# A hybrid attention layer on one core: gate rows by sums on VectorE, and another order of the first loads

## The reference, cut to what matters

```
shift, scale, gate = split(silu(cond) @ w_ada + b_ada, 3)     # cond: c_ctx for context, c for latents
h = rms_norm(x, g_norm) * (1 + scale) + shift
z = h @ w_in                                                  # q, k, v, g of both mixers
oa = differential attention, 8 heads: (softmax1 - lam * softmax2) @ v
ob = grouped-query attention, 8 heads, q and k RMS-normalised
o  = concat(rms_norm(oa) * silu(ga), ob * silu(gb))
y  = rms_norm(x + gate * (o @ w_out), g_final)
```

## Time and profile before

| | us |
|---|---|
| median of 3 runs | 1323.68 (1323.24 to 1323.74) |
| the profiled execution | 1324.19, span 1322.3 |
| TensorE matmul busy in the span | 1267.9 |
| VectorE busy | 717.7 |
| ScalarE busy | 601.9 |
| GpSimd busy | 217.0 |

### The profile page before, as it was taken

How to read it: one execution, slowest core, us unless ns; L and a number is a source line. 1 busy time by engine, 2 the same in 40 slices (tenths; PEclk the granted TensorE clock), 3 DMA queues, 4 the chain that set the end, 5 groups by cost and what they waited for, 6 DMA issues and landing times.

```text
span 1322.3 us, 19007 instructions
## 1 busy us (share of the span) xinstructions
PE 1267.9 (96%) x7399; PEld 1017.3 (77%) x7399; DVE 717.7 (54%) x1155; ACT 601.9 (46%) x1265; POOL 217.0 (16%) x374
## 2 busy tenths in 40 slices
PE   2699999999999999999999999999999999999996
PEld 1466666788888888888888787878788787888885
DVE  1444441855647657456565656565666766523343
ACT  1322312454555545555555545555555656322123
POOL 2000110301202003022122222121213322200001
PEclk9999999999999999999999999999999999999998
DMA  9999784211212112131212222221213431433234
GB/s 300 359 354 350 272 270 161 65 47 50 68 49 84 33 53 88 49 91 53 78 57 78 73 63 71 60 81 57 86 49 108 126 108 64 150 121 135 80 135 159
DMA packets 144216, 156.57 MB, mean 118 GB/s; under 512 B 8008, under 2 KB 122792, under 8 KB 143360
## 3 DMA queue, kind: packets, MB, share of 16 engines
q1 hardware_dynamic: 137232, 132.19, 31.1%
q0 software_dynamic: 6896, 23.17, 5.5%
HBM read 144.18 MB, written 11.16 MB: 117 GB/s over the span
## 4 chain that ended last, share of the span: by engine, by line
PE 88%; DVE 5%; DMA 3%; SPq 2%; ACT 1%; issue 1%; POOL 0%; ACTq 0%; DVEq 0%
PE z_ps L542 23%; PE z_ps L544 22%; PE z_ps L543 22%; PE ring L637 5%; PE ring L738 5%; PE ring L672 3%; PE ring L740 2%; PE ring L562 2%; SPq L455 1%; DMA x_sb<-in_x_sample_dram 1%; PE ring L764 1%; PE ring L544 1%; PE ring L543 1%; PE ring L542 1%; DMA ada_raw<-in_w_ada_dram 1%; DMA w_raw<-in_w_in_dram 1%
## 5 line engine op out<-in xcount | busy, mean ns | idle before, releaser
L542 PE MATMUL z_ps<-w_hi,xt_hi 128*128 128x512 f32 x1360 | 567.5, 417 | 2.4 <-DVE xt_lo L1270 1.0
L544 PE MATMUL z_ps<-w_hi,xt_lo 128*128 128x512 f32 x1360 | 533.2, 392 | 0.0
L543 PE MATMUL z_ps<-w_lo,xt_hi 128*128 128x512 f32 x1360 | 531.5, 391 | 0.0
L1126 DVE TENSOR_TENSOR w_lo<-w_raw,w_hi 128x512 fp32r<-128x512 f32 x272 | 191.6, 707 | 249.0 <-ACT w_hi L814 247.0
L814 ACT ACTIVATE w_hi<-w_raw 128x512 fp32r<-128x512 f32 x272 | 170.4, 627 | 335.0 <-PE z_ps L544 322.2
L542 PEld LDWEIGHTS z_ps<-w_hi,xt_hi 128*128 128x128 f32 x1360 | 256.1, 188 | 69.9 <-issue 23.7
L544 PEld LDWEIGHTS z_ps<-w_hi,xt_lo 128*128 128x128 f32 x1360 | 255.5, 188 | 56.9
L543 PEld LDWEIGHTS z_ps<-w_lo,xt_hi 128*128 128x128 f32 x1360 | 257.4, 189 | 37.8
L922 ACT ACTIVATE s_sb<-s_sb,small 128x768 f32<-128x768 f32 (+1 forms) x120 | 97.9, 820 | 2.8 <-DVE small L1206 2.8
L1206 DVE TENSOR_REDUCE small<-s_sb 128x2 f32<-128x1536 f32 (+1 forms) x60 | 88.3, 1471 | 18.7 <-ACT s_sb L814 17.5
L738 PE MATMUL ring<-v_hl,pt_hi 128*128 128x256 f32 x400 | 96.2, 324 | 0.0
(11 more groups left out here) (147 smaller groups left out, 1257.4 us busy)
## 6 DMA issues: line engine op xcount, KB each, us to landing
w_raw<-in_w_in_dram SPq DMA_DIRECT2D x208, 256.0 KB, 3.1
ada_raw<-in_w_ada_dram SPq DMA_DIRECT2D x64, 512.0 KB, 8.8
w_raw<-in_w_out_dram SPq DMA_DIRECT2D x64, 256.0 KB, 3.5
gate_pt<-in_w_ada_dram SPq DMA_DIRECT2D x12, 512.0 KB, 6.6
gate_sg<-in_w_ada_dram SPq DMA_DIRECT2D x12, 512.0 KB, 5.4
o_spill<-row_st POOLq DMA_DIRECT2D x14, 320.0 KB, 3.1
row_st<-o_spill POOLq DMA_DIRECT2D x14, 320.0 KB, 3.4
x_sb<-in_x_sample_dram SPq DMA_DIRECT2D x4, 1024.0 KB, 13.6
```

The costliest lines, as they stand in the source:

```text
L542: pe.matmul(out, hi_l, hi_r, start=start, stop=False)
L543: pe.matmul(out, hi_l, lo_r, start=False, stop=False)
L544: return pe.matmul(out, lo_l, hi_r, start=False, stop=stop)
L1126: dve.tensor_tensor(w_lo[:, b, :], w_raw[:, kg // 2 % RAW_RING, kg % 2, :], w_hi[:, b, :].bitcast(F32), ALU.subtract).then_inc(w_lo_done, 1)
```

## The change

It does two things.

1. *Order of the first loads.* SP issues the five token tiles first, then modulation weights 0 to 3. TensorE transposes the tokens of step 0 before its first modulation products, and VectorE normalises the tokens before it handles the first modulation rows. GpSimd issues the `lam` tables only when six slices of `xt_lo` are done and the norm and rotation tables when twelve are; the work on them on ScalarE and VectorE moves from step 3 to step 8 and, for the norm weight, step 15.

2. *The gate.* The 64 products of passes 0 and 1 go. The gate columns are loaded in passes 6 to 12 by GpSimd, two buffers of 512 KB, into the half of the work area that mixer A leaves unused (the tiles q, k, v, pt are laid out by halves for that). In steps 4, 9, 11 and 13 VectorE multiplies 512 columns by a column of silu(cond) and adds them to `gate_acc`, once for each of the two rows: `gate_sums`, 64 parts of two instructions, ten parts in a pass (`GATE_STEPS`). What then lies over 128 partitions is summed by eight products at the end of step 0 of pass 13 (`step_gate`); the bias is added in step 1 of that pass, where before it was pass 2. The bias is loaded in pass 5 instead of pass 1. Two waits of ScalarE and VectorE on the gate's bank in pass 2 go.

```diff
-GATE_SLOT = KT - 3
-GATE_END = 2 * KT - 1
-GATE_RING = 8
+GATE_COLS = D_MODEL // 2
+GATE_LOADS = 2 * KT
+GATE_STEPS = [4, 4, 9, 9, 11, 11, 13, 13, 13, 13]
+GATE_FROM = 4
+GATE_SUM_IT = OUT_IT
...
+def gate_parts():
+
+    out, i = {}, 0
+    for it in range(D_IT + 1, GATE_SUM_IT):
+        for s in GATE_STEPS:
+            if i < 2 * GATE_LOADS and (it, s) >= (D_IT + 1, GATE_FROM):
+                out.setdefault((it, s), []).append(i)
+                i += 1
+    return out
...
-            for n in range(4):
-                load_ada(n)
             for t in range(TILES):
                 src = x_prompt[0] if t == 0 else xs_v[:, t - 1, :]
                 sp.dma_start(x_sb[:, t, :], src).then_inc(x_in[t], 16)
+            for n in range(4):
+                load_ada(n)
+            load_w(0)
             load_ada(4)
-            load_w(0)
             load_w(1)
...
-            def step_gate(s):
+            def step_gate():
+
                 n = TURN["GATE"]
-                bank = claim(n) if s == GATE_SLOT else RB(n)
-                for m in gate_pieces(s):
-                    k, u = divmod(m, 2)
-                    pe.wait_ge(gate_in[m % GATE_RING], 16 * (m // GATE_RING + 1))
-                    for jj in range(2):
...
+                bank = claim(n)
+                pe.wait_ge(sel_set, 4)
+                pe.wait_ge(gate_summed, 2 * GATE_LOADS)
+                for r in range(2):
+                    for j in range(4):
+                        ins = pe.matmul(bank[32 * j:32 * j + 2, :], gate_sel[:, r, :],
+                                        gate_acc[:, r, NCOL * j:NCOL * (j + 1)], start=(r == 0), stop=(r == 1))
+                filled(ins, n)
+
+            h_transpose(0, 0)
             for quarter in range(4):
                 modulation(0, quarter)
             columns(0)
-            h_transpose(0, 0)
             h_transpose(0, 1)
...
+            def gate_sums(i):
+
+                m, piece = divmod(i, 2)
+                k, u = divmod(m, 2)
+                dve.wait_ge(gate_in[u], 16 * (k + 1))
+                if k:
+                    dve.wait_ge(gate_summed, i - 3)
+                raw = gate_raw[:, u, NCOL * piece:NCOL * (piece + 1)]
+                c0 = GATE_COLS * u + NCOL * piece
+                for r in range(2):
+                    acc, weight = gate_acc[:, r, c0:c0 + NCOL], cs[:, KT * r + k:KT * r + k + 1]
+                    if k == 0:
+                        ins = dve.tensor_scalar(acc, raw, weight, None, ALU.mult)
+                    else:
+                        ins = dve.scalar_tensor_tensor(acc, raw, weight, acc, ALU.mult, ALU.add)
+                ins.then_inc(gate_summed, 1)
...
-                    if it == G_IT + 1 and s == 0:
+                    if (it, s) == (GATE_SUM_IT, 1):
                         gate_rows_out()
+                    for i in GATE_PARTS.get((it, s), []):
+                        gate_sums(i)
...
+            pool.wait_ge(h_lo, KT // 2 - 2)
             for i, v_ in enumerate((lam_q1, lam_q2, lam_k1, lam_k2)):
                 pool.dma_start(lam_raw[:, i, :], v_.rearrange("a h d -> a (h d)").broadcast_to([P, H_A * DK_A])
                                ).then_inc(lam_in, 16)
+            pool.wait_ge(h_lo, KT - 4)
...
+                    for i in past:
+                        if i % 2 and i // 2 + 2 < GATE_LOADS:
+                            pool.wait_ge(gate_summed, i + 1)
+                            load_gate(i // 2 + 2)
+                    past = GATE_PARTS.get((it, s), [])
```

## The result

The changed kernel takes 1335.0 us (median of 4 runs, 1334.6 to 1335.7) against 1323.7 (4 runs, 1323.2 to 1324.1) of the kernel before on the same chip: ratio 1.0085, interval 1.0072 to 1.0098. It is 11.3 us slower; 6.1 were forecast. The profiled execution took 1335.7 us with a span of 1333.8. Further down, one of four executions of `e3_even` had a granted clock of 0.56 throughout and took 2080 us, and the times given for that run are those of the other three.

What follows compares the result with a forecast made beforehand. A start set by loads, then TensorE's own queue, was taken to bound the kernel. The terms -21.2 + 1.6 + 3.7 - 1.2 + 2.0 - 5.0 + 25.2 + 1.0 gave +6.1 us: 1329.8 on the median, range 1323 to 1337.

Steps and rivals of the forecast that it cites:

- passes 6 to 12: VectorE's gate sums delay pt_lo and TensorE waits: 2.8 us in pass 6, 3.8 each in 7 to 11, together +25.2.
- pass 13: Eight last gate products cost +2.0 us; four additions ahead of v_lo and q_lo on VectorE cost +1.0.
- The gate groups: Passes 0 and 1: dropping 18 groups of gate products saves TensorE 1.18 us each, -21.2 us.
- The rotation's wait: Start of pass 1: without four covering gate groups, the transposes of k wait for the rotated z, +3.7 us.
- The duration of a sum: VectorE, passes 6 to 12: one operation on 128x512 takes 0.66 us from start to start.
- S4: Step 9: two parts ahead of pt_lo make the TensorE products that claim its banks stall 1.0 us.
- V4: Step 13: four parts ahead of pt_lo make the TensorE products that need it stall 2.3 us.
- The 0.5 for GpSimd: Step 13: three small GpSimd operations beside the four parts slow VectorE, +0.5 us (0 to 0.9).
- Passes 6 and 12: Pass 6 costs 2.8 us with cheap first parts; pass 12 costs 3.4, of it 2.65 at S4 and 0.7 in step 4.
- the start: Pass 0: tokens first, small tables moved into the modulation stream at a cost of 5.5 us; gain -5.0 us (-2.6 to -9).
- the start doesn't move: Rival, pass 0: tables in the saturated stream cost what they did before, -5 becomes -1; 1334 us, 12%.
- sums fit: Rival, passes 6 to 12: VectorE, busy 54%, has room for the sums, so all of +25.2 goes; 1304.6 us, 12%.

Runs made afterwards that it cites:

- e3_even: Changed kernel with the 64 parts of the gate sums two each behind steps 4, 6, 8, 10 and 12 of a pass; 1317.5 us, ratio 0.9944.
- e7_qk5: Changed kernel with sums behind steps 4, 6, 10, 12, 14 and pass 1's transposes of k in step 5 instead of 3; 1305.5 us, ratio 0.9855.
- e10_old_order: Changed kernel, sums behind steps 4, 6, 10, 12, 14, 15, small tables behind modulation weights, k transposes in step 5, first modulation weights ahead of tokens; 1299.2 us.
- e6_tables_last: Changed kernel with sums behind steps 4, 6, 10, 12, 14 and all small tables loaded behind the last modulation weights; 1305.3 us, ratio 0.9855.
- e1_start: Kernel before with only the new start: token tiles first, small tables inside pass 0, gate products left in passes 0 and 1; 1322.7 us, ratio 0.9983.
- e5_free: Changed kernel with the 64 parts of the gate sums two each behind steps 4, 6, 10, 12 and 14 of a pass; 1309.3 us, ratio 0.9884.
- e2_sums: Changed kernel with the old start, so that only the gate's way is changed; 1339.2 us, ratio 1.0111.
- e4_lam_late: Changed kernel with the lambda tables loaded with the norms, behind step 12 of pass 0; 1336.3 us, ratio 1.0092.

## Where the prediction was right and wrong

The measured 1335.0 us lie inside the forecast's 1323 to 1337, and the mechanism of passes 6 to 12 was forecast wait by wait. That the number is no further off is in part luck: a start that gained 2.8 us less than forecast and a pass 1 that gained 1.0 less are made up by stalls 3.2 us smaller and a pass 13 that costs 1.1 less, and the half clock of passes 6 to 12 was in no term.

The forecast's terms by place, against the table of passes:

| place | forecast | measured | of it half clock |
|---|---|---|---|
| start, to the last modulation group | -5.0 | -2.2 | not told apart |
| gate groups and xt_lo waits, end of pass 0 | -1.9 | -1.5 | |
| pass 1 | -14.0 | -13.0 | 0 |
| pass 2 | -1.2 | -1.7 | |
| passes 6 to 12 | +25.2 | +28.1 | +6.1 |
| pass 13 | +3.0 | +1.9 | |
| sum | +6.1 | +11.6 | |

- **The gate groups** were 1.19 us each (pass 1's plain steps went from 4.59 to 3.40), forecast 1.18. **The rotation's wait** is 3.8 us, forecast 3.7. `e7_qk5` shows that it is the missing cover: with two more steps of products ahead of the transposes it is gone. That the wait for `k_lo` behind it grows by 1.0 us was in no term.
- **The duration of a sum**, 0.66 us from start to start, came from two other shapes and an overlap of 0.09; it measured 0.66. The next operation starts 0.08 before the end of the one before it, so the rule of the Trainium skill (VectorE: DVE Perf Modes, The DRAIN you can't avoid), by which it would start only when that one has emptied, does not fit these rows; the same section names the case that does, a next operation that isn't held and starts earlier. The six passes did not cost the 6 us more.
- **S4** waits 1.00 us, forecast 1.0. **V4** makes its step 2.51 us longer, forecast 2.3 + 0.5. The 0.5 for GpSimd was wrong at this place: its root lies inside the eight sums of 690.49 to 695.79, which take no longer for it. It is GpSimd that takes longer: 0.40 and 0.96 us for the same operations that take 0.19 and 0.55 at 674.3 to 675.1, for another tile.

```profile
692.88 0.40 POOL L1423 TENSOR_SCALAR small<-small 128x1 f32<-128x1 f32 x1 [4.94 <-ACT sq_o L934]
693.36 0.96 POOL L1424 TENSOR_TENSOR small<-small,half 128x1 f32<-128x1 f32 x1
```

  In step 4 GpSimd's products on 128x128 run beside four sums, which take 646.77 - 643.75 = 3.02 us instead of 2.65; nobody waits there.

```profile
643.75 3.09 DVE L1317 SCALAR_TENSOR_TENSOR gate_acc<-gate_raw,cs,gate_acc 128x512 f32<-128x512 f32 x4
646.77 0.68 DVE L1116 TENSOR_TENSOR w_lo<-w_raw,w_hi 128x512 fp32r<-128x512 f32 x1
...
643.64 0.46 POOL L1484 TENSOR_TENSOR sg<-sg,zs 128x128 f32<-128x128 f32 x1 [9.82 <-DVE sg L1176]
644.18 0.79 POOL L1487 TENSOR_TENSOR sg<-sg,norms 128x128 f32<-128x128 f32 x1
```

  GpSimd works there for 1.25 us and VectorE loses 0.37; GpSimd's second product takes 0.79 us instead of 0.46. By the Trainium skill (SBUF — State Buffer, Who interferes with whom) it is the issue order that decides who blocks. These rows agree so far: what I had put down to VectorE alone falls on GpSimd in step 13 and on both in step 4. Whether one blocks the other in full they don't settle.
- **Passes 6 and 12**: without their half clock 5.41 - 3.0 = 2.4 and 3.82 - 1.55 = 2.3 us, forecast 2.8 and 3.4. In pass 12 I added 0.7 for step 4, which isn't there, and let all of 2.65 count; S4's wait grew from 1.1 to 3.4. The stalls of the seven passes come to 2.4 + 5 x 3.45 + 2.3 = 22 us, 3 less than forecast.
- **The failed step is the start**: "The tables are moved into that stream and cost it 1.6 MB / 353 = 4.5 us, up to 6.5". I priced the tables by their bytes and took 5.5. They cost it some 7: with the tables inside, the stream's rate falls at 132 to 134 us, as in the kernel before (192 GB/s), and with the tables behind it at 126 to 128 (47 GB/s in `e10_old_order`, which has the old order), where the changed kernel still moves 348. The changed kernel, then `e6_tables_last`:

```profile
132.00:134.00 2.00, 2.00 (x12) 1.47 (x10) 0.69 (x1) 1.07 (x2) 0.00 (x0) 1.00 0.45 162
```

```profile
126.00:128.00 2.00, 2.00 (x34) 1.53 (x23) 0.94 (x2) 0.29 (x1) 0.00 (x0) 1.00 0.14 50
```

  So the tables cost inside the stream what they had cost ahead of it, and the stream ends no earlier. What is left is that TensorE, 2.7 us behind the stream before, now keeps up with it: 2.2 us (`e1_start`: 2.0), under even my lower bound of 2.6. The rival "the start doesn't move" had this mechanism, at 12%, with a gain of 1 us; its 1334 us is the nearest number of them all, though it has no clock in it either. That the price is more than the bytes' has two visible parts, the low rates of 85 to 87 us and SyncE's issues of 2.9 to 5.7 us behind the tables, where 1.85 is usual. Why those issues take longer no run here tells.
- **The missing term is the clock**: I read it as 1.00 in every window, though the first product in the earlier trace rows takes 0.79 us and not 0.50 or 0.40 as those of the earlier trace rows, and added waits of 2.3 and 3.7 us to a TensorE that had had none inside its passes, without asking what its clock does behind them. In passes 6, 9 and 12 that is 3.0 + 1.55 + 1.55 = 6.1 us, more than the whole miss of 5.5 in the sum.
- **Pass 13**: the new products take 1.90 us, forecast 2.0; the additions ahead of v_lo and q_lo cost nothing, where I took 1.0.
- **The rival "sums fit"** was right in its core: VectorE has the room, as `e5_free` shows. What the given order lacks is the place, which was the argument against the rival.

## What to carry to other kernels

Work is free on an engine with idle time only where no consumer stands close behind the next instruction in its queue: before placing it, walk from the inserted work through everything queued behind it to each waiting product, and take the step whose consumer is farthest. When a change puts waits of 2 us or more into an engine that ran without any, add a term for its clock behind each. Price a load in a saturated stream by what the same load cost where it stood before, not by its bytes, and put it behind the stream rather than at another place inside it.

## What was not expected of the hardware

- Behind waits from 1.7 us on (pass 12 of `e7_qk5`), TensorE ran at half clock for 3.4 to 6.8 us, for some of these waits and not for others of the same length, and for different ones in two executions. The longest wait inside the passes without one is the 3.76 us for the rotation in `e2_sums`. Behind the waits of 1.0 us in front of S4 (5 in each of four traces) and of 1.3 in passes 7 to 11 of `e3_even` it never did. So the length of a wait alone doesn't tell.
- The granted clock of the windows doesn't show all of it. At the start of the kernel before it reads 1.00 in every window, here at 50 to 52 us. But 32 modulation products take 1.89 us at 43.95 and again at 50.34, as they do in `e4_lam_late` at 132.91, where the granted clock is 0.50, and 1.06 from 53.32 on; the products between follow at 0.43 us instead of 0.23.

```profile
50.00:52.00 2.00, 2.00 (x33) 0.99 (x32) 0.00 (x0) 0.00 (x0) 0.00 (x0) 1.00 1.10 349
```

```profile
43.95 1.89 PE L562 MATMUL ring<-ada_raw,cs 128*2 128x128 f32 x32
...
47.22 0.63 PE L543 MATMUL z_ps<-w_lo,xt_hi 128*128 128x512 f32 x1
...
53.32 1.06 PE L562 MATMUL ring<-ada_raw,cs 128*2 128x128 f32 x32
```

  `e2_sums` and `e10_old_order`, which have the old order too, show the same pace up to 50 and 43 us at a granted clock of 1.00. So the kernel before did run at the pace of the lower level behind its waits at the start, and the duration of a known instruction tells it where the granted clock does not.
- Loads that send the same 2 KB to 128 partitions lower the rate of a saturated stream (238 and 124 GB/s in two windows with the DMA engines busy, where weights move at some 350) and hold up SyncE's issues behind them (5.66 us for two instead of 1.85). Of the engines' busy share in such short windows not every number can be taken as it stands: it is 1.86 at 86 to 87 us.
